# Freeing the buffers of split weights by half tiles, in a four-layer trunk on one core

## The chip, the cores and the metric

The kernel runs on one core of a Trainium2 chip. The metric is the device time of one launch in microseconds (us); the median of several runs is compared.

## The reference, cut to what matters

Four layers on a residual stream of 256 tokens by 1024 channels, float32. Each layer has a token mixer and then a conv-gated MLP:

```
for i in range(4):
    h = rms_norm(x, norm_mix[i])
    y = [dsa_mixer, rwkv7_mixer, s5_mixer][i % 3](h, ...)   # layers 0 and 3: dsa
    x = x + y
    h = rms_norm(x, norm_ffn[i])
    u = conv3(h @ w_up) + conv_b            # w_up: 1024 x 5632, causal depthwise, width 3
    gate, val = split(u); x = x + (silu(gate) * val) @ w_down   # w_down: 2816 x 1024
```

The DSA mixer projects queries, keys, values and an indexer (`dsa_w_in`), takes for each query the top 64 keys by indexer score, does attention over them with normed queries and keys, and projects with `dsa_w_out`.

## The kernel before

The residual is kept transposed, `xT`: 128 channels per block on partitions, 8 blocks, 256 tokens. Every weight matrix is walked in tiles of 1024 rows by 256 columns (`TILE`), that is two blocks (b = 0, 1) of 128 output channels and 8 chunks of the inner dimension. A tile fills one psum bank, block 0 the first half of it and block 1 the second. SyncE loads the tiles into a ring of three slots (`ring`, `send`, `wait_slot`).

Most weights are split in two fp32r parts, high and low, and a product is three matmuls (`product`, L386 to L390: high by high, high by low, low by high). The split is made on the chip, block by block:

- ScalarE copies the raw block to `w_high` (`round_weights`, L363), both blocks one after the other;
- VectorE subtracts for block 0 and GpSimd for block 1 into `w_low` (`rest_of_weights`, L371), each when `w_rounded` of the block says so;
- TensorE waits for `w_split` of the block (`split_weights`).

There are two buffers for split tiles (`NSPLIT` = 2). So tile n + 2 overwrites the parts of tile n, and ScalarE waits until tile n is wholly multiplied (`wait_used`, mostly the semaphore `bank_full` of its psum bank). `ahead(split, eng, key, ...)` issues the split of the tile two after `key`. Every engine works in its own program order, which is written out by hand:

- In `project` and `mlp_pe` TensorE does block 0's eight chunks and then block 1's, 24 matmuls each. Where the inputs come one by one (`ready`, the first tile of a stage, and the first and third tile of an MLP) the blocks alternate chunk by chunk.
- The MLP's up tiles come in pairs j (gate tile h = 0, value tile h = 1). For each, `mlp_act` waits for the tile, scales it by the newest tap (L769) and then rounds the weights ahead; `mlp_dve` adds the other taps (L846), does the low part ahead of block 0, and after both tiles multiplies gate and value (L857). `mlp_pool` does block 1's low part and the low part of the inner activations (L798).
- The down stage has 4 column groups m with 3 row groups g each, 8, 8 and 6 chunks. In layer 1, VectorE computes tables for the next layer's S5 mixer between its low parts (`add_down`, `s5_tables`).
- In the DSA stage the tiles are i0, i1, an unsplit s, then k0 to k3, q0 to q3, v0 to v3, o0 to o3. ScalarE evicts each with a Square and a Copy behind the rounding (`evict_k`, `evict_q`, `evict_v`); TensorE needs the squares halfway through the next tile for the mean of each head (L954, L969). VectorE weighs the indexer's heads (L1238, L1240), finds the top keys (L1249, L1250, L1254), norms the keys (L1228, L1230), masks scores (L1265) and normalises (L1286), with the low parts at fixed places between. `project_tokens` does the value tiles with tokens as rows: both blocks of the weights are read by every product.
- `add_residual` adds an output tile to `xT` (L565), does a low part ahead, and prepares the input of the MLP (`split_early`, L429, `add_squares`, L440).
- At the start of a stage `norm_scale` (L483, L488) makes the normed input chunk by chunk, with ScalarE's `norm_round` (L503), and with a low part of weights after chunk 3.

Of the kernel before, what the change touches and what calls it, by code (L numbers as in the profile page):

```python
# [33 lines left out]
DC = D // P  # L34
# [76 lines left out]
class Plan:  # L111


    def __init__(self):
        self.tiles = []
        self.tile = {}
        self.used = {}
        self.split = {}
        self.split_tiles = []
        self.slot_dmas = [0] * NSLOT  # L120
        self.fills = [0] * NBANK
        self.bank = {}

    def weights(self, key, dmas=1, split=False):
        if split:
            self.split[key] = len(self.split_tiles)
            self.split_tiles.append(key)
        n = len(self.tiles)
        slot = n % NSLOT
        self.slot_dmas[slot] += 16 * dmas  # L130
        self.tiles.append(key)
        self.tile[key] = (n, slot, self.slot_dmas[slot])
# [51 lines left out]
def trunk(nc, A, out, layers=(0, 1, 2, 3)):  # L184
    plan = make_plan(layers)
    ctx = ExitStack()
    with ctx:
# [157 lines left out]

        def rows_of(key):
            return min(DC, FC - key[3] * DC) if key[1] == "down" else DC
# [7 lines left out]
        def round_weights(act, key, r=0):  # L355

            n = plan.split[key]
            w = landed(act, key, r)
            if n >= NSPLIT:
                wait_used(act, plan.split_tiles[n - NSPLIT], r)  # L360
            for b in range(2):
                raw, high, _ = split_part(key, b, w)
                act.activation(high, raw, ACT.Copy).then_inc(sem("w_rounded", b), 1)  # L363
# [152 lines left out]
        def project(pe, key, x, ready=None, halfway=None):  # L516
# [4 lines left out]
            for k, b in chunks_and_blocks(DC, ready):  # L521
# [7 lines left out]
                if key in plan.split:  # L529
                    mm = product(pe, out_, (parts[b][0][:, k, :], parts[b][1][:, k, :]), (x[0][:, k, :], x[1][:, k, :]),  # L530
                                 start, stop)
                else:
                    mm = pe.matmul(out_, parts[b][:, k, b * P:(b + 1) * P], x[:, k, :], start=start, stop=stop,  # L533
                                   skip_group_check=True)
# [25 lines left out]
        def add_residual(dve, L, s):  # L560

            for m in range(4):
                wait_full(dve, (L, s, m))
# [3 lines left out]
                if m < 3:  # L567
                    ahead(rest_of_weights, dve, (L, s, m), 0)
# [123 lines left out]
        def mlp_pe(pe, L):  # L692
# [3 lines left out]
            def pair(j, r):  # L696
                for h in range(2):
# [11 lines left out]
                    for c, b in chunks_and_blocks(DC, first):  # L709
                        if first and b == 0:  # L710
                            early_ready(pe, n, c) if j == 0 else wait_split_h(pe, n, c)
                        if b not in parts:
                            parts[b] = split_weights(pe, key, b, r)
                        mm = product(pe, banks[bank][:, b * T:(b + 1) * T], (parts[b][0][:, c, :], parts[b][1][:, c, :]),
                                     (high[:, c, :], low[:, c, :]), c == 0 and (b == 0 or not first), c == DC - 1)
                    mm.then_inc(sem("bank_full", bank), 1)
# [6 lines left out]
            for m in range(4):  # L723
                for g in range(3):
# [3 lines left out]
                    for b in range(2):  # L728
# [5 lines left out]
                        for k in range(kn):  # L734
# [8 lines left out]
                            else:  # L743
                                mm = product(pe, banks[bank][:, 0:T], (high[:, k, :], low[:, k, :]),
                                             (inner_high[:, c, :], inner_low[:, c, :]), first, last)
                        if g == 2:
                            mm.then_inc(sem("bank_full", bank), 1)
# [3 lines left out]
        def mlp_act(act, L):  # L751
# [5 lines left out]
            def pair(j, r):  # L757
# [3 lines left out]
                for h in range(2):  # L761
                    key = (L, "up", 2 * j + h)
                    if j:
                        wait_full(act, key, r)
                    else:
                        act.wait_ge(sem("scaled"), h + 1 + since("scaled", L))
# [5 lines left out]
                    if j:  # L772
                        ahead(round_weights, act, key, r=r)
# [48 lines left out]
        def mlp_dve(dve, L):  # L822
            def pair(j, r):
# [8 lines left out]
                for h in range(2):  # L832
                    bank = bank_of((L, "up", 2 * j + h))
# [16 lines left out]
                    if j:  # L850
                        ahead(rest_of_weights, dve, (L, "up", 2 * j + h), 0, r=r)
# [228 lines left out]
        def dsa_act(act, L):  # L1080
# [7 lines left out]
            def evict_k(i):  # L1088

                key = (L, "k", i)  # L1090
                wait_full(act, key)
                ahead(round_weights, act, key)
# [6 lines left out]
            def evict_q(g):  # L1099

                key = (L, "q", g)
                wait_full(act, key)
                ahead(round_weights, act, key)
# [14 lines left out]
            def evict_v(i):  # L1118

                key = (L, "v", i)  # L1120
                wait_full(act, key)
                ahead(round_weights, act, key)
# [1793 lines left out]
```

## Time and profile before

| | |
|---|---|
| runs | 1569.55, 1571.79, 1573.05 us; median 1571.79 |
| profiled execution | span 1570.8 us, first to last instruction; the profile gives no other time for it |
| TensorE busy | 1437.3 us, 92% |
| VectorE busy | 1073.6 us, 68% |
| ScalarE busy | 764.2 us, 49% |
| GpSimd busy | 643.2 us, 41% |
| DMA | 210.09 MB, mean 134 GB/s |
| mean granted TensorE clock | 0.966 |

PE is TensorE, DVE VectorE, ACT ScalarE, POOL GpSimd. The span of the profiled execution lies 1.0 us under the median of the runs. Matmuls are pipelined, so that TensorE's busy time counts more than the array's work, and a short wait between two of them doesn't show as idle time. A row of a timeline gives the start, the duration (of all that it merges, x2 for two), the engine, the line and the operation, and in brackets the idle time of the engine before it with what ended it.

### The profile page before, as it was taken

Reading aid. Unit: us, or ns where it says so; the run is one execution under the profiler, and the core shown is the slowest. Engines: PE = TensorE matmul, PEld = TensorE weight load, DVE = VectorE, ACT = ScalarE, POOL = GpSimd, SP = SyncE. Lnnn points to the kernel's source line nnn. Section 1 sums busy time; section 2 is a strip of 40 time slices with the busy share of each in tenths; the row PEclk is TensorE's granted clock in tenths of the full one; section 3 lists DMA queues with packets and bytes.
Section 4 is the critical chain, followed back from the end, with each engine's and each line's share of the span. In section 5 each row is a group of like instructions: output and inputs, shape, how many; then the busy total and the mean of one; then the engine's idle time right before and its main releaser. Section 6 shows DMA issues by size and latency. Waiting matters only on the chain.

```text
span 1570.8 us, 32850 instructions
## 1 busy us (share of the span) xinstructions
PE 1437.3 (92%) x13742; PEld 1344.1 (86%) x13742; DVE 1073.6 (68%) x1635; ACT 764.2 (49%) x1229; POOL 643.2 (41%) x319
## 2 busy tenths in 40 slices
PE   6989999999999888999997547999999898999998
PEld 5888999988787777999987547999989788999998
DVE  6496677743585556877798995687744598577652
ACT  4358565542251334655643103565655357565542
POOL 5232357752005203487640001457664232257753
PEclk8899999999999999999999768999999999999999
DMA  5443445553434002475551002545555343445553
GB/s 160 137 134 106 134 162 188 181 191 112 134 109 134 5 4 66 151 215 187 173 170 61 1 1 82 162 161 188 187 168 180 123 135 108 134 148 177 186 194 101
DMA packets 212053, 210.09 MB, mean 134 GB/s; under 512 B 12098, under 2 KB 211058, under 8 KB 211922
## 3 DMA queue, kind: packets, MB, share of 16 engines
q1 hardware_dynamic: 210784, 206.65, 40.9%
q0 software_dynamic: 800, 1.46, 0.5%
q8 instruction: 99, 1.62, 0.5%
q14 instruction: 32, 0.26, 0.1%
q10 hardware_dynamic: 338, 0.10, 0.0%
HBM read 207.15 MB, written 1.05 MB: 133 GB/s over the span
## 4 chain that ended last, share of the span: by engine, by line
PE 68%; DVE 23%; ACT 5%; issue 3%; POOL 1%; DMA 0%; ACTq 0%; DVEq 0%; SPq 0%; POOLq 0%
PE psum L388 14%; PE psum L390 13%; PE psum L389 13%; PE psum L739 7%; PE psum L533 5%; DVE work L2394 4%; DVE w_low L371 4%; PE psum L741 3%; ACT w_high L363 3%; DVE x_low L488 1%; DVE work L483 1%; DVE work L1228 1%; DVE work L846 1%; PE psum L1596 1%; PE psum L1610 1%
## 5 line engine op out<-in xcount | busy, mean ns | idle before, releaser
L371 POOL TENSOR_TENSOR w_low<-ring,w_high 128x1024 fp32r<-128x1024 f32 (+1 forms) x185 | 512.9, 2773 | 791.6 <-ACT w_high L363 746.9
L388 PE MATMUL psum<-x_high,w_high 128*128 128x256 f32 x1856 | 533.3, 287 | 14.6 <-DVE w_low L371 9.7
L389 PE MATMUL psum<-x_low,w_high 128*128 128x256 f32 x1856 | 527.9, 284 | 0.0
L390 PE MATMUL psum<-x_high,w_low 128*128 128x256 f32 x1856 | 527.9, 284 | 0.0
L363 ACT ACTIVATE w_high<-ring 128x1024 fp32r<-128x1024 f32 (+1 forms) x368 | 362.1, 1035 | 215.0 <-PE psum L390 125.3
L388 PEld LDWEIGHTS psum<-x_high,w_high 128*128 128x128 f32 x1856 | 359.0, 193 | 21.3 <-issue 14.4
L389 PEld LDWEIGHTS psum<-x_low,w_high 128*128 128x128 f32 x1856 | 359.0, 193 | 1.0 <-issue 1.0
L390 PEld LDWEIGHTS psum<-x_high,w_low 128*128 128x128 f32 x1856 | 359.0, 193 | 0.0
L371 DVE TENSOR_TENSOR w_low<-ring,w_high 128x1024 fp32r<-128x1024 f32 x183 | 249.1, 1362 | 130.3 <-ACT w_high L363 130.0
L846 DVE SCALAR_TENSOR_TENSOR work<-psum,par,work 128x255 f32<-128x255 f32 (+1 forms) x352 | 145.0, 476 | 119.7 <-ACT work L769 119.6
L739 PE MATMUL psum<-inner,w_high 128*128 128x512 f32 x528 | 186.4, 398 | 2.6 <-DVE w_low L371 2.6
L769 ACT ACTIVATE work<-psum,par 128x256 f32<-128x256 f32 x176 | 89.3, 561 | 174.0 <-PE psum L390 174.0
L741 PE MATMUL psum<-inner,w_low 128*128 128x256 f32 x528 | 148.1, 280 | 0.0
L739 PEld LDWEIGHTS psum<-inner,w_high 128*128 128x128 f32 x528 | 99.1, 188 | 27.2 <-DVE w_low L371 2.3
L857 DVE TENSOR_TENSOR work<-work 128x512 f32<-128x512 f32 x44 | 118.4, 2690 | 0.4
L741 PEld LDWEIGHTS psum<-inner,w_low 128*128 128x128 f32 x528 | 99.7, 189 | 0.0
L533 PE MATMUL psum<-work,ring 128*128 128x256 f32 x384 | 85.9, 381 | 2.1 <-DVE work L1918 1.1
L533 PEld LDWEIGHTS psum<-work,ring 128*128 128x128 f32 x384 | 72.2, 190 | 16.0 <-DVE work L1918 3.7
L798 POOL TENSOR_TENSOR inner<-work,inner 128x512 f32 (+1 forms) x44 | 75.0, 1709 | 0.0
L2394 DVE TENSOR_TENSOR work<-work 128x32 f32<-128x32 f32 (+5 forms) x108 | 67.9, 628 | 4.3 <-ACT work L2200 1.4
L388 PE MATMUL psum<-early_high,w_high 128*128 128x256 f32 x192 | 55.8, 291 | 3.7 <-DVE work L2600 1.9
L389 PE MATMUL psum<-early_low,w_high 128*128 128x256 f32 x192 | 54.3, 283 | 0.0
(322 smaller groups left out, 2126.7 us busy)
## 6 DMA issues: line engine op xcount, KB each, us to landing
ring<-in_ffn_w_up_dram SPq DMA_DIRECT2D x88, 1024.0 KB, 5.1
ring<-in_ffn_w_down_dram SPq DMA_DIRECT2D x32, 1024.0 KB, 5.0
ring<-in_dsa_w_in_dram SPq DMA_DIRECT2D x28, 1024.0 KB, 5.3
ring<-in_ffn_w_down_dram SPq DMA_DIRECT2D x16, 768.0 KB, 4.3
ring<-in_rwkv_w_rkv_dram SPq DMA_DIRECT2D x12, 1024.0 KB, 5.0
ring<-in_dsa_w_out_dram SPq DMA_DIRECT2D x8, 1024.0 KB, 5.0
ring<-in_s_w_glu_dram SPq DMA_DIRECT2D x8, 1024.0 KB, 5.3
ring<-in_rwkv_w_out_dram SPq DMA_DIRECT2D x4, 1024.0 KB, 5.0
```

Source lines behind the costliest of these rows:

```text
L363: act.activation(high, raw, ACT.Copy).then_inc(sem("w_rounded", b), 1)
L371: eng.tensor_tensor(low, raw, high.bitcast(F32), ALU.subtract).then_inc(sem("w_split", b), 1)
L388: pe.matmul(out_, lhs[0], rhs[0], start=start, stop=False, skip_group_check=True)
L389: pe.matmul(out_, lhs[0], rhs[1], start=False, stop=False, skip_group_check=True)
L390: return pe.matmul(out_, lhs[1], rhs[0], start=False, stop=stop, skip_group_check=True)
L533: mm = pe.matmul(out_, parts[b][:, k, b * P:(b + 1) * P], x[:, k, :], start=start, stop=stop, skip_group_check=True)
L739: pe.matmul(banks[bank][:, :], high[:, k, :], inner[:, :, c, :], start=first, stop=False, skip_group_check=True)
L741: mm = pe.matmul(banks[bank][:, 0:T], low[:, k, :], inner_high[:, c, :], start=False, stop=last, skip_group_check=True)
L769: act.activation(conv[:, j % 3, h, b, :], bank_of(key)[:, b * T:(b + 1) * T], ACT.Identity, bias=col("ffn_conv_b", c + L * 2 * FC, r), sca ...
L846: dve.scalar_tensor_tensor(out=row, in0=bank[:, b * T:(b + 1) * T - lag], scalar=col("ffn_conv_w", c + (L * 3 + tap) * 2 * FC, r), in1=row ...
L857: dve.tensor_tensor(gated[:, j % 3], conv[:, j % 3, 0], conv[:, j % 3, 1], ALU.mult).then_inc(sem("gated_done"), 1)
L2394: then(dve.tensor_tensor(out_, x, y, op))
```

## The change

Three things change. The plan gives each split tile a number in a new count, `half`, save value tiles and the third row group of the down stage, and TensorE increments `tile_half` with the last product that reads block 0. `round_weights` takes the blocks to do; for block 0 it waits for `tile_half` of the tile two before (for the third row group of the down stage: for the psum bank of its block 0; for value tiles: for the whole tile, as before), and for block 1 for the whole tile. And the order on two engines is changed: in the up loop and in `evict_k`, `evict_q` and `evict_v`, ScalarE rounds block 0 ahead of its wait for the tile and block 1 behind it (in the up loop behind the scaled tap as well); in the up loop and in `add_residual`, VectorE does its low part ahead of the taps or of the addition rather than behind them.

```diff
@@ Plan.weights
+            if key[1] != "v" and key[1:2] + key[3:] != ("down", 2):
+                self.half[key] = len(self.half) + 1
@@ new helpers
+        def wait_half(eng, key, r=0):
+            if key in plan.half:
+                eng.wait_ge(sem("tile_half"), r * ROUND + plan.half[key])
+            elif key[1] == "down":
+                wait_full(eng, (key[0], "down", key[2], 0))
+            else:
+                wait_used(eng, key, r)
+        def half_done(key, mm, last_of_first):
+            if last_of_first and key in plan.half:
+                mm.then_inc(sem("tile_half"), 1)
@@ round_weights
-        def round_weights(act, key, r=0):
+        def round_weights(act, key, *blocks, r=0):
             n = plan.split[key]
             w = landed(act, key, r)
-            if n >= NSPLIT:
-                wait_used(act, plan.split_tiles[n - NSPLIT], r)
-            for b in range(2):
+            for b in blocks or range(2):
+                if n >= NSPLIT:
+                    (wait_used if b else wait_half)(act, plan.split_tiles[n - NSPLIT], r)
                 raw, high, _ = split_part(key, b, w)
                 act.activation(high, raw, ACT.Copy).then_inc(sem("w_rounded", b), 1)
@@ project (mlp_pe alike, with c for k; in the down stage on b == 0)
+                    half_done(key, mm, b == 0 and k == DC - 1)
@@ add_residual
+                if m < 3:
+                    ahead(rest_of_weights, dve, (L, s, m), 0)
                 wait_full(dve, (L, s, m))
...
-                if m < 3:
-                    ahead(rest_of_weights, dve, (L, s, m), 0)
@@ mlp_act, for each tile of a pair
                     if j:
+                        ahead(round_weights, act, key, 0, r=r)
                         wait_full(act, key, r)
...
                     if j:
-                        ahead(round_weights, act, key, r=r)
+                        ahead(round_weights, act, key, 1, r=r)
@@ mlp_dve, for each tile of a pair
+                    if j:
+                        ahead(rest_of_weights, dve, (L, "up", 2 * j + h), 0, r=r)
                     bank = bank_of((L, "up", 2 * j + h))
...
-                    if j:
-                        ahead(rest_of_weights, dve, (L, "up", 2 * j + h), 0, r=r)
@@ evict_k (evict_q and evict_v alike)
+                ahead(round_weights, act, key, 0)
                 wait_full(act, key)
-                ahead(round_weights, act, key)
+                ahead(round_weights, act, key, 1)
```

## Rows read from the trace of the kernel before

**Rows 1.** The page's busy times: engine, busy us, share of the span, instructions.

```profile
PE 1437.3 (92%) x13742; PEld 1344.1 (86%) x13742; DVE 1073.6 (68%) x1635; ACT 764.2 (49%) x1229; POOL 643.2 (41%) x319
```

**Rows 2.** The chain that ended last, 88 to 125 us: start, us, what.

```profile
88.62 3.23 DVE w_low L371
...
112.79 3.33 DVE w_low L371
```

**Rows 3.** Timeline of the up loop: start us, us, engine, line, operation, idle before.

```profile
216.66 1.02 ACT L769 ACTIVATE work<-psum,par 128x256 f32<-128x256 f32 x2 [2.78 <-PE psum L390]
...
222.43 1.02 ACT L769 ACTIVATE work<-psum,par 128x256 f32<-128x256 f32 x2 [2.84 <-PE psum L390]
...
225.05 1.22 DVE L371 TENSOR_TENSOR w_low<-ring,w_high 128x1024 fp32r<-128x1024 f32 x1
...
225.42 3.11 POOL L371 TENSOR_TENSOR w_low<-ring,w_high 128x1024 fp32r<-128x1024 f32 x1 [2.66 <-ACT w_high L363]
```

**Rows 4.** Timeline of the start of the MLP of layer 0, by engine.

```profile
197.79 0.36 PE L388 MATMUL psum<-x_high,w_high 128*128 128x256 f32 x1 [1.52 <-DVE w_low L371]
...
210.62 0.38 PE L388 MATMUL psum<-x_high,w_high 128*128 128x256 f32 x1 [0.73 <-DVE w_low L371]
...
190.60 2.01 ACT L363 ACTIVATE w_high<-ring 128x1024 fp32r<-128x1024 f32 x2 [2.46 <-PE psum L390]
...
192.69 2.41 POOL L371 TENSOR_TENSOR w_low<-ring,w_high 128x1024 fp32r<-128x1024 f32 x1 [3.19 <-ACT w_high L363]
...
192.95 2.43 DVE L488 TENSOR_TENSOR x_low<-work,x_high 128x256 fp32r<-128x256 f32 x1 [2.10 <-ACT x_high L503]
...
207.48 2.00 ACT L363 ACTIVATE w_high<-ring 128x1024 fp32r<-128x1024 f32 x2
...
209.35 1.21 DVE L371 TENSOR_TENSOR w_low<-ring,w_high 128x1024 fp32r<-128x1024 f32 x1
...
209.56 6.62 POOL L371 TENSOR_TENSOR w_low<-ring,w_high 128x1024 fp32r<-128x1024 f32 x2 [3.49 <-ACT w_high L363]
```

**Rows 5.** Timeline of TensorE in the DSA stage of layer 0.

```profile
57.53 1.10 PE L954 MATMUL psum<-work,mean_head 128*128 128x512 f32 x2 [0.37 <-ACT work L1096]
...
75.05 1.13 PE L954 MATMUL psum<-work,mean_head 128*128 128x512 f32 x2 [0.27 <-ACT work L1096]
...
106.42 0.72 PE L985 MATMUL psum<-work 64*128 64x128 f32 x8 [1.37 <-DVE work L1265]
...
116.99 0.66 PE L996 MATMUL psum<-ident,work 128*128 128x128 f32 x4 [1.88 <-DVE work L1286]
```

**Rows 6.** Timeline of ScalarE, VectorE and GpSimd in the DSA stage of layer 0.

```profile
62.89 2.01 ACT L363 ACTIVATE w_high<-ring 128x1024 fp32r<-128x1024 f32 x2 [2.04 <-PE psum L390]
...
86.31 2.01 ACT L363 ACTIVATE w_high<-ring 128x1024 fp32r<-128x1024 f32 x2 [2.26 <-PE psum L390]
...
64.10 1.22 DVE L371 TENSOR_TENSOR w_low<-ring,w_high 128x1024 fp32r<-128x1024 f32 x1
...
64.98 2.59 POOL L371 TENSOR_TENSOR w_low<-ring,w_high 128x1024 fp32r<-128x1024 f32 x1 [6.04 <-ACT w_high L363]
...
81.25 2.43 POOL L371 TENSOR_TENSOR w_low<-ring,w_high 128x1024 fp32r<-128x1024 f32 x1 [4.61 <-ACT w_high L363]
...
81.67 3.10 DVE L371 TENSOR_TENSOR w_low<-ring,w_high 128x1024 fp32r<-128x1024 f32 x1
...
103.05 2.24 DVE L1254 TENSOR_SCALAR work<-work 128x256 f32<-128x256 f32 x1
```

**Rows 7.** Timeline of layer 1: its up loop and its down stage.

```profile
691.81 0.39 PE L388 MATMUL psum<-x_high,w_high 128*128 128x256 f32 x1 [0.24 <-POOL w_low L371]
...
789.21 1.23 DVE L371 TENSOR_TENSOR w_low<-ring,w_high 128x1024 fp32r<-128x1024 f32 x1 [1.41 <-ACT w_high L363]
...
817.31 1.23 DVE L371 TENSOR_TENSOR w_low<-ring,w_high 128x1024 fp32r<-128x1024 f32 x1 [0.79 <-ACT w_high L363]
...
845.63 0.69 DVE L589 TENSOR_TENSOR xT<-xT,psum 128x512 f32<-128x512 f32 x1
```

More of the change, by code:

```diff
@@ L119, in __init__ @@
         self.split_tiles = []
+        self.half = {}
         self.slot_dmas = [0] * NSLOT
@@ L715, in pair @@
                                      (high[:, c, :], low[:, c, :]), c == 0 and (b == 0 or not first), c == DC - 1)
+                        half_done(key, mm, b == 0 and c == DC - 1)
                     mm.then_inc(sem("bank_full", bank), 1)
@@ L745, in mlp_pe @@
                                              (inner_high[:, c, :], inner_low[:, c, :]), first, last)
+                        half_done((L, "down", m, g), mm, b == 0)
                         if g == 2:
@@ L1101, in evict_q @@
                 key = (L, "q", g)
+                ahead(round_weights, act, key, 0)
                 wait_full(act, key)
-                ahead(round_weights, act, key)
+                ahead(round_weights, act, key, 1)
                 if g < 2:
@@ L1120, in evict_v @@
                 key = (L, "v", i)
+                ahead(round_weights, act, key, 0)
                 wait_full(act, key)
-                ahead(round_weights, act, key)
+                ahead(round_weights, act, key, 1)
                 act.activation(v_tok[:, :, i * TILE:(i + 1) * TILE],
```

## The prediction

> **What bounds the kernel now.** I read the page first. TensorE is busy for 92% of the span [rows 1], so at most 133 us of idle time is there to win, and I looked for where it sits. Next the timeline of the up loop [rows 3]. ScalarE starts the scaled tap of one tile at 216.66 us and of the next at 222.43: a tile of 48 products takes 5.76 us, 0.12 us a product. VectorE finishes the low part of block 0 at 226.3 (225.05 + 1.22) and GpSimd that of block 1 at 228.5 (225.42 + 3.11). TensorE takes them up at about 228.2 and 231.1. Nothing waits: in this loop weights are ready 1.9 to 2.6 us early, and readying them sooner is worth nothing. The same view, for TensorE alone and over the whole span, gives the places where it does wait. A row's "idle" understates them: a product is drawn 0.28 us long but they follow each other at 0.12, so an idle of x costs x + 0.16. The places are: the first tiles of each of the four MLPs [rows 4], the DSA stage of layers 0 and 3 [rows 5], one tile of layer 1's up loop and its down stage [rows 7]. In the DSA stage the chain that ended last runs through VectorE from 88.6 to 125 us, and its low parts of weights are steps of it, 3.2 and 3.3 us each [rows 2]; the instruction alone takes 1.2 [rows 6]. The RWKV and S5 cores hold most of the other idle time and the change doesn't touch them.
>
> **How VectorE and GpSimd meet.** This decides the DSA stage. GpSimd's low part takes 2.4 us. Where VectorE's falls into it (81.67 in a GpSimd run from 81.25 to 83.68) it ends 1.08 us after GpSimd does [rows 6]: it waited, and then ran. So do its tensor_scalar at 103.05 (2.24 us) [rows 6] and its x_low at 192.95 (2.43 us, behind GpSimd's run from 192.69) [rows 4]. In the other direction GpSimd's 3.11 us at 225.42 holds the 0.75 us that VectorE still had to run [rows 3]. Each such meeting costs the later one up to 2.4 us. The Trainium skill (SBUF — State Buffer, "SBUF: two separate sides") says the two share a port pair as an exclusive lock, which goes for a whole instruction to whichever starts first. That speaks against counting the change as free, since it moves GpSimd's runs.
>
> **The change, part by part.** No instruction of work is added or removed; one semaphore increment rides on an existing product, and one wait takes the place of another.
>
> *ScalarE's block 0 leaves the end of a tile.* Its two copies took 2.00 us for both behind the tile's end. Block 0 now starts at half of the tile, 2.88 us earlier, when ScalarE is idle; block 1 starts 0.95 earlier than it did, and with it GpSimd. In the up loop and in the down stages of layers 0, 2 and 3 this adds slack where there was slack: 0 us. If that cover were gone (a low part over 2 us late) it would cost what is over; nothing in the rows comes near. SP frees a ring slot when both low parts are done, about 1 us sooner; loads are not waited for now, so 0.
>
> *Start of an MLP, third tile (197.79, idle 1.52).* Tile 0 interleaves its blocks, so block 0 ends only three products, 0.36 us, before the tile. ScalarE starts at 190.24 rather than 190.60, GpSimd at 192.33 rather than 192.69, VectorE's x_low waits for it as before, and all behind moves by 0.36. Bounds: 0 to 0.5. Four MLPs: 1.4; the first index tiles of the two DSA layers have the same form: 0.7. Sum 2.1 us.
>
> *Start of an MLP, fifth tile (210.62, idle 0.73, so 0.9 lost).* VectorE's low part stands behind the four taps of the third tile and runs from 209.35. Now ScalarE rounds block 0 before the two instructions of its tap (0.9 to 1.0 us, as in [rows 3], just ahead of its 207.48), so from 206.58 to 207.6, and VectorE's part ends at 208.9; TensorE comes at 209.6 and doesn't wait. Block 1 is what is late next: ScalarE has it at 209.5 as before, GpSimd runs 209.6 to 212.0 (its run was longer because VectorE's low part held it), and TensorE wants it at 212.4. It holds by 0.4. The taps start some 1.3 us later; their readers aren't near. Gain 0.9 × 4 = 3.6, bounds 0.5 × 4 and 0.9 × 4 [rows 4].
>
> *Layer 1, 691.81 (idle 0.24).* GpSimd was late with block 1, after its own DMA issues; it starts its chain 1 us earlier: 0.4 [rows 7].
>
> *Layer 1's down stage.* VectorE computes S5 tables between the low parts and ends the stage (addition at 845.63). It waited for ScalarE's rounding 1.41 us at 789.21 and 0.79 at 817.31 [rows 7]. ScalarE's block 0 is 1 us earlier at the first and far earlier at the second: 1.0 + 0.8, and one meeting with GpSimd gets 0.2 shorter: 2.0. Bounds: 0.5 (one whole meeting more on this chain would take 2.4 of it, less what it moves) to 3.
>
> *DSA, key and query tiles.* The head means wait for ScalarE's copies behind the rounding: idle 0.37 once and 0.27 four times [rows 5]. One copy of 1 us leaves that queue, against 0.43 to 0.53 lost, so all five close: 0.53 + 4 × 0.43 = 2.25 us a layer, if nothing else fills them. Something does. VectorE is the slower engine here, so I follow its order. Logits come 0.53 earlier, and it is ready for the low part of k1's successor at 63.57 (64.10 before). GpSimd, at 64.98 before, moves by 0.53 and by the 0.95 of the one copy, to 63.49 [rows 6]. It takes the port 0.08 us ahead and VectorE is done at 67.0, 1.7 later than now. The next low part meets GpSimd's 72.6 to 75.0 and ends at 76.1. Weighing then starts at 79.2, just as GpSimd's run for q1 does (79.3), and its products wait for 81.95; it ends at 85.75, and q1's low part at 86.9. TensorE wants q1 at 84.8 (q0 ends just before ScalarE's 86.31 now, and 0.53 and two times 0.43 are won by then): a stall of 2.2 us that wasn't there. From here TensorE is 0.85 later than before. But the meetings that VectorE had at 88.62, 7.3 later and at 103.05 change: the first is gone (90.85 to 92.0), the second ends at 99.2 as before, the third at 104.4 rather than 105.3. The wait for the mask at 106.42 (1.37) shrinks and TensorE is 0.9 earlier; a shorter meeting before the wait at 116.99 brings 0.4 more. So 1.3 a layer, 2.6 for both. Value tiles keep their wait for the whole tile, and the output tiles run without idle time: 0. Bounds: −2.4 a layer (one more meeting on the chain than counted, with the 1.3 lost half) and +4.5.
>
> The Trainium skill's rule would give the same here, to whoever is first: by it the two are 0.08 us apart, and no row decides between them with more than that. If it went the other way the sum would be the case B below.
>
> **The sum.** 2.1 + 3.6 + 0.4 + 2.0 + 2.6 = 10.7 us off the profiled span of 1570.8: 1560.1. The median of the runs, 1571.8, stands 1.0 above that span, so 1561.1; I give 1561.0.
>
> **Rivals.**
> A, the above: 1561.0.
> B, *VectorE gets in first at 63.5.* Then its low part ends at 64.7 and it is 2.3 ahead; weighing is cut by one run of GpSimd, q1's low part ends at 83.5 (wanted at 84.8, no stall), two later meetings remain, and the mask is ready at 103.35 rather than 106.4. The five gaps and most of the wait at 106.42 are kept: 3.4 a layer. 8.1 + 6.9 = 15: 1556.8; if the later waits for masks close too, a further 1 a layer, 1554.8. For it: only 0.08 us stands against it, less than ScalarE's or TensorE's hand-over times vary between rows. Against it: both layers have the same spacing, so it has to tip twice.
> C, *the late part becomes another.* At the fifth tile GpSimd's block 1 has 0.4 us to spare; if VectorE's next low part holds it, the 0.9 is lost again (−3.6). The S5 tables meet one more run of GpSimd (−2.0), and the DSA chain gives back its 2.6. What is left is 2.5: 1569.3, no measurable change. In favour: six meetings are near at hand in rows 4 and 6. Against: three independent places must fail.
> D, *slower.* One mechanism: in the DSA stage GpSimd's run, now 1 us after the tile's end rather than 2, falls on VectorE's weighing of the second query half, on the low part before it and on that behind it, in each round. A lost port is 2.4 us, and VectorE sets this stage. To cancel 10.7 and cost 3 more, each layer must lose about 7 us, three meetings more than in A. Time then 1575. For it: the sequence has a dozen such instructions and I count margins of 0.1 us. Against: a VectorE that is late passes into stretches where GpSimd is idle for 4.6 us and more, which limits how many it can lose.
> E, *the change doesn't act*, because block 0 is still rounded behind the tile: excluded for single-block order, and true for the interleaved tiles, where I count only 0.36.
>
> **How the numbers follow.** A 0.47, B 0.31, C 0.13, D 0.09. What a measurement of this kernel can tell from no change is 0.2%, 3.1 us, so 1568.6 is the border: faster holds A, B and a part of C's spread, 0.82; same 0.11; slower 0.07. The range goes from B's lower end with a little beyond (1554) to C's edge (1568.5); below it lies some of B, above it C and D, together under 2 in 10. A's own range is 1558 to 1565.
>
> **What the profile after would show.** Right: TensorE's idle before the fifth tile of each MLP gone, the third tile's down to 1.16; ScalarE's L363 as single instructions, one at half of a tile and one at its end; the gaps before the head means gone; in layer 1's down stage VectorE without a wait for L363 at 817 and its last addition about 2 us earlier against the stage's start. For A: TensorE waits about 2.2 us for q1's low part. For B: it doesn't, and the wait at 106.42 is 0.6. Wrong would be: new waits of TensorE on GpSimd's low part at an MLP's fifth tile, or low parts of VectorE over 3 us at more places in the DSA stage than the five of now.

## The result

The changed kernel takes 1559.68 us (median of 4 runs, 1558.62 to 1562.13) against 1571.0 before. The ratio is 0.992, with a 95% interval of 0.9903 to 0.9936: 0.8% faster. The prediction said 1561.0. The profiled execution took 1560.63 us with a span of 1558.9, 11.9 less than before, with a mean granted clock of 0.963.

Line numbers move: `round_weights` is L380, `rest_of_weights` L388, `product` L405 to L407, the scaled tap L790, the other taps L869; the kernels of the experiments have numbers a few lines off these. First the page's busy times, to be read against [rows 1], and two of its groups (busy us, mean ns of one, then idle time before and its releaser), with the same two groups of the kernel before at the end:

```profile
PE 1436.8 (92%) x13742; PEld 1346.4 (86%) x13742; DVE 1099.2 (71%) x1635; ACT 772.5 (50%) x1229; POOL 585.2 (38%) x319
...
L388 POOL TENSOR_TENSOR w_low<-ring,w_high 128x1024 fp32r<-128x1024 f32 (+1 forms) x185 | 454.3, 2456 | 836.0 <-ACT w_high L380 791.4
...
L388 DVE TENSOR_TENSOR w_low<-ring,w_high 128x1024 fp32r<-128x1024 f32 x183 | 302.3, 1652 | 154.3 <-ACT w_high L380 153.2
```

```profile
L371 POOL TENSOR_TENSOR w_low<-ring,w_high 128x1024 fp32r<-128x1024 f32 (+1 forms) x185 | 512.9, 2773 | 791.6 <-ACT w_high L363 746.9
...
L371 DVE TENSOR_TENSOR w_low<-ring,w_high 128x1024 fp32r<-128x1024 f32 x183 | 249.1, 1362 | 130.3 <-ACT w_high L363 130.0
```

GpSimd is 58 us less busy and VectorE 26 us more. No work moved between them; the time in which one holds the other is drawn as busy time of the one that is held. More often now it is VectorE: its low parts grew by 53 us and GpSimd's shrank by 59, while VectorE's products of gate and value, less held than before, went from 118.4 to 80.6 us. At most places nothing is late for it.

The start of layer 0's MLP, TensorE, ScalarE, VectorE and GpSimd in turn, to be read against [rows 4]:

```profile
191.41 0.36 PE L405 MATMUL psum<-x_high,w_high 128*128 128x256 f32 x1 [1.17 <-DVE w_low L388]
...
200.21 1.04 ACT L380 ACTIVATE w_high<-ring 128x1024 fp32r<-128x1024 f32 x1
...
202.06 2.00 ACT L380 ACTIVATE w_high<-ring 128x1024 fp32r<-128x1024 f32 x2
...
201.41 1.22 DVE L388 TENSOR_TENSOR w_low<-ring,w_high 128x1024 fp32r<-128x1024 f32 x1
...
204.11 2.58 DVE L388 TENSOR_TENSOR w_low<-ring,w_high 128x1024 fp32r<-128x1024 f32 x1
...
203.19 2.42 POOL L388 TENSOR_TENSOR w_low<-ring,w_high 128x1024 fp32r<-128x1024 f32 x1 [3.49 <-ACT w_high L380]
```

The third tile waits 1.17 us instead of 1.52, and the fifth no longer waits: its low part of block 0 is done at 202.6, ahead of the taps. The next one, at 204.11, starts inside GpSimd's run and takes 2.58, and nothing is late for it.

Further into the up loop, VectorE and GpSimd, to be read against [rows 3]:

```profile
243.18 2.31 DVE L388 TENSOR_TENSOR w_low<-ring,w_high 128x1024 fp32r<-128x1024 f32 x1
...
247.83 1.71 DVE L388 TENSOR_TENSOR w_low<-ring,w_high 128x1024 fp32r<-128x1024 f32 x1 [0.78 <-ACT w_high L380]
...
246.05 2.41 POOL L388 TENSOR_TENSOR w_low<-ring,w_high 128x1024 fp32r<-128x1024 f32 x1 [1.65 <-ACT w_high L380]
```

Here GpSimd holds VectorE's low part in every tile: it takes 2.31 and 1.71 us in turn, where it took 1.22 before. It stands ahead of the taps now, and ends 4.1 and 5.9 us before TensorE takes up its tile (245.49 for about 249.6, 249.54 for about 255.4), where it was 1.9 us before. So these meetings cost nothing.

The DSA stage of layer 0, TensorE, VectorE and GpSimd, to be read against [rows 5] and [rows 6]:

```profile
53.29 1.02 PE L975 MATMUL psum<-work,mean_head 128*128 128x512 f32 x2
...
82.96 0.36 PE L405 MATMUL psum<-x_high,w_high 128*128 128x256 f32 x1 [2.15 <-DVE w_low L388]
101.41 0.72 PE L1006 MATMUL psum<-work 64*128 64x128 f32 x8 [0.43 <-DVE work L1289]
111.39 0.66 PE L1017 MATMUL psum<-ident,work 128*128 128x128 f32 x4 [1.27 <-DVE work L1310]
...
59.79 3.41 DVE L388 TENSOR_TENSOR w_low<-ring,w_high 128x1024 fp32r<-128x1024 f32 x1
...
75.75 5.61 DVE L1264 SCALAR_TENSOR_TENSOR work<-work 128x256 f32<-128x256 f32 x7
...
81.59 1.22 DVE L388 TENSOR_TENSOR w_low<-ring,w_high 128x1024 fp32r<-128x1024 f32 x1
...
59.72 2.41 POOL L388 TENSOR_TENSOR w_low<-ring,w_high 128x1024 fp32r<-128x1024 f32 x1 [5.50 <-ACT w_high L380]
...
75.46 2.50 POOL L388 TENSOR_TENSOR w_low<-ring,w_high 128x1024 fp32r<-128x1024 f32 x1 [4.22 <-ACT w_high L380]
```

This is case A. The head means don't wait (no bracket at 53.29). GpSimd starts 0.07 us ahead of VectorE at 59.7, and VectorE's low part ends 1.07 us after GpSimd's. That puts the weighing (75.75) behind GpSimd's next run, q1's low part ends at 82.8, and TensorE waits 2.15 us for it. Layer 3 has the same row at 1264.49, also 2.15.

Layer 1's down stage, TensorE and then VectorE, against [rows 7]:

```profile
789.58 0.50 PE L758 MATMUL psum<-inner,w_high 128*128 128x512 f32 x1 [0.83 <-DVE w_low L388]
...
823.21 0.39 PE L405 MATMUL psum<-inner,w_high 128*128 128x256 f32 x1 [0.94 <-DVE w_low L388]
...
762.62 1.65 DVE L869 SCALAR_TENSOR_TENSOR work<-psum,par,work 128x255 f32<-128x255 f32 x4 [1.29 <-ACT work L790]
...
811.10 1.23 DVE L388 TENSOR_TENSOR w_low<-ring,w_high 128x1024 fp32r<-128x1024 f32 x1
...
833.95 0.69 DVE L607 TENSOR_TENSOR xT<-xT,psum 128x512 f32<-128x512 f32 x1
```

Where the 11.9 us came from, with each boundary the start of a row in both traces (the first row of the s tile, the first head mean, the first product of each MLP and of layer 1's mixer, the first taps of the last up tile, the last addition):

| stretch | before | after | difference |
|---|---|---|---|
| start to layer 0's s tile | 34.75 | 34.09 | −0.66 |
| to its first head mean | 22.78 | 19.20 | −3.58 |
| rest of its DSA mixer | 126.09 | 124.32 | −1.77 |
| MLP of layer 0 | 203.57 | 202.22 | −1.35 |
| layer 1's mixer and up loop | 384.16 | 382.79 | −1.37 |
| layer 1's down stage | 74.28 | 71.33 | −2.95 |
| layer 2's mixer | 168.53 | 167.99 | −0.54 |
| layer 2's MLP, to layer 3's s tile | 211.48 | 211.16 | −0.32 |
| to its first head mean | 19.69 | 21.73 | +2.04 |
| rest of its DSA mixer | 126.07 | 125.98 | −0.09 |
| MLP of layer 3, to the end | 199.4 | 198.09 | −1.31 |

Two of these are not the change's work but the clock's. The windows of the two stretches from s tile to head mean, before and then after (the last three columns are the granted clock as a share of 2.4 GHz, the DMA share and GB/s):

```profile
34.75:57.53 22.78, 22.41 (x123) 20.84 (x123) 4.72 (x5) 4.28 (x9) 6.75 (x4) 0.72 0.44 140
1225.64:1245.33 19.69, 19.33 (x122) 18.21 (x123) 5.88 (x8) 6.39 (x11) 3.54 (x2) 0.84 0.52 161
```

```profile
34.09:53.29 19.20, 19.20 (x122) 18.27 (x123) 4.66 (x5) 4.31 (x9) 7.82 (x7) 0.83 0.52 164
1213.10:1234.83 21.73, 21.73 (x123) 20.56 (x123) 5.79 (x8) 6.39 (x11) 3.97 (x2) 0.73 0.47 146
1004.00:1006.00 2.00, 2.00 (x11) 2.00 (x11) 1.75 (x3) 1.97 (x3) 0.00 (x0) 0.50 0.00 0
1266.00:1268.00 2.00, 2.00 (x12) 2.00 (x11) 1.86 (x7) 0.00 (x0) 0.59 (x1) 0.50 1.01 350
```

In both layers TensorE waits 4.2 to 5.0 us ahead of the s tile, in both kernels, and then runs a part of the stretch at 1.2 GHz (in the kernel before, the granted clock is 0.50 from 34 to 40 and from 46 to 50). A stretch of t us at a granted clock c lacks t(1 − c) us of full clock: layer 0's 6.4 before and 3.3 after, layer 3's 3.2 and 5.9. That is −3.1 and +2.7 of the table's −3.58 and +2.04; what is left is −0.5 and −0.7, the head mean's wait of 0.53 that is gone. The same stretch with the same work differs by 3 us between two layers of one execution, so this is not to be credited to the change, and over both layers it nearly cancels.

### The profile page after: what moved, and what is told of

Same layout as the page of the kernel before. It is cut to its first block, busy times and chain, and to the rows that moved or that the text cites. A ratio compares the mean times of both kernels' runs of the same rounds, so it can differ in the third digit from the quotient of the medians.

```text
span 1558.9 us, 32946 instructions
## 1 busy us (share of the span) xinstructions
PE 1436.8 (92%) x13742; PEld 1346.4 (86%) x13742; DVE 1099.2 (71%) x1635; ACT 772.5 (50%) x1229; POOL 585.2 (38%) x319
## 4 chain that ended last, share of the span: by engine, by line
PE 73%; DVE 22%; ACT 3%; issue 2%; DMA 0%; ACTq 0%; DVEq 0%; SPq 0%
PE psum L405 16%; PE psum L407 15%; PE psum L406 15%; PE psum L758 6%; PE psum L551 5%; DVE work L2418 4%; PE psum L760 3%; DVE w_low L388 3%; DVE x_low L505 2%; DVE work L500 1%; DVE work L1252 1%; ACT w_high L380 1%; DVE work L1264 1%; PE psum L1620 1%; PE psum L1634 1%
## 5 line engine op out<-in xcount | busy, mean ns | idle before, releaser
L388 POOL TENSOR_TENSOR w_low<-ring,w_high 128x1024 fp32r<-128x1024 f32 (+1 forms) x185 | 454.3, 2456 | 836.0 <-ACT w_high L380 791.4
L405 PE MATMUL psum<-x_high,w_high 128*128 128x256 f32 x1856 | 532.9, 287 | 12.9 <-DVE w_low L388 9.5
L407 PE MATMUL psum<-x_high,w_low 128*128 128x256 f32 x1856 | 527.8, 284 | 0.0
L380 ACT ACTIVATE w_high<-ring 128x1024 fp32r<-128x1024 f32 (+1 forms) x368 | 376.8, 1037 | 224.1 <-PE psum L407 132.6
L388 DVE TENSOR_TENSOR w_low<-ring,w_high 128x1024 fp32r<-128x1024 f32 x183 | 302.3, 1652 | 154.3 <-ACT w_high L380 153.2
L405 PEld LDWEIGHTS psum<-x_high,w_high 128*128 128x128 f32 x1856 | 358.8, 193 | 18.6 <-issue 13.9
L407 PEld LDWEIGHTS psum<-x_high,w_low 128*128 128x128 f32 x1856 | 358.8, 193 | 0.0
L869 DVE SCALAR_TENSOR_TENSOR work<-psum,par,work 128x255 f32<-128x255 f32 (+1 forms) x352 | 144.6, 472 | 46.7 <-ACT work L790 46.5
L790 ACT ACTIVATE work<-psum,par 128x256 f32<-128x256 f32 x176 | 89.3, 561 | 131.7 <-PE psum L407 131.7
L878 DVE TENSOR_TENSOR work<-work 128x512 f32<-128x512 f32 x44 | 80.6, 1831 | 6.9 <-DVE work L869 5.1
L405 PE MATMUL psum<-early_high,w_high 128*128 128x256 f32 x192 | 56.4, 294 | 3.5 <-DVE work L2624 1.9
L407 PE MATMUL psum<-early_high,w_low 128*128 128x256 f32 x192 | 55.0, 287 | 0.0
```

Source lines behind the costliest of these rows:

```text
L388: eng.tensor_tensor(low, raw, high.bitcast(F32), ALU.subtract).then_inc(sem("w_split", b), 1)
L405: pe.matmul(out_, lhs[0], rhs[0], start=start, stop=False, skip_group_check=True)
L407: return pe.matmul(out_, lhs[1], rhs[0], start=False, stop=stop, skip_group_check=True)
L790: act.activation(conv[:, j % 3, h, b, :], bank_of(key)[:, b * T:(b + 1) * T], ACT.Identity, bias=col("ffn_conv_b", c + L * 2 * FC, r), sca ...
L869: dve.scalar_tensor_tensor(out=row, in0=bank[:, b * T:(b + 1) * T - lag], scalar=col("ffn_conv_w", c + (L * 3 + tap) * 2 * FC, r), in1=row ...
L878: dve.tensor_tensor(gated[:, j % 3], conv[:, j % 3, 0], conv[:, j % 3, 1], ALU.mult).then_inc(sem("gated_done"), 1)
```

## The experiments

Eight kernels in two groups, each timed in five rounds beside the kernel before: its median was 1571.95 in the first group (1 to 4), 1570.62 in the second (5 to 8).

### 1. ScalarE's half alone

The changed kernel with VectorE's order of before.

```diff
@@ add_residual and mlp_dve
-                    if j:
-                        ahead(rest_of_weights, dve, (L, "up", 2 * j + h), 0, r=r)
                     bank = bank_of((L, "up", 2 * j + h))
                     ...
+                    if j:
+                        ahead(rest_of_weights, dve, (L, "up", 2 * j + h), 0, r=r)
```

> The changed kernel with VectorE's order of before: low parts behind taps and additions, ScalarE as changed. My theory: VectorE's order matters only at the fifth tile of each MLP (0.9 us each), so this is 3.6 us slower than the changed kernel, about 1563.3, with the idle of 0.7 before the fifth tile back. Rival, that order is worth nothing (block 0 rounded earlier by ScalarE is enough): 1559.7.

Measured: 1585.51 us (1582.36 to 1591.07), ratio 1.0093 (1.0076 to 1.0111). This was missed by 22 us and on the wrong side: half of a change that wins 0.8% loses 0.9%. Its timeline, TensorE at the fifth tile, then ScalarE, VectorE and GpSimd in the up loop:

```profile
208.73 0.38 PE L405 MATMUL psum<-x_high,w_high 128*128 128x256 f32 x1 [3.18 <-DVE w_low L388]
...
216.28 1.02 ACT L790 ACTIVATE work<-psum,par 128x256 f32<-128x256 f32 x2 [1.88 <-PE psum L407]
...
228.06 1.02 ACT L790 ACTIVATE work<-psum,par 128x256 f32<-128x256 f32 x2 [1.97 <-PE psum L407]
...
224.66 2.92 DVE L388 TENSOR_TENSOR w_low<-ring,w_high 128x1024 fp32r<-128x1024 f32 x1
...
224.08 2.42 POOL L388 TENSOR_TENSOR w_low<-ring,w_high 128x1024 fp32r<-128x1024 f32 x1 [3.35 <-ACT w_high L380]
```

ScalarE now has block 1 a microsecond sooner, so GpSimd starts at 224.08 while VectorE is at its taps, and VectorE's low part at 224.66 takes 2.92 us and not 1.22. In [rows 3] it was VectorE that started first, by 0.37 us. Without VectorE's new order, the 1.9 us by which TensorE had its weights early are used up: a pair of tiles takes 11.78 us (228.06 − 216.28) instead of 11.52 (two of 5.76), and the fifth tile waits 3.18, in the other layers 3.20, 3.20 and 3.21. Ten pairs of 0.26 and one wait of 3.2 + 0.16 are 6.0 us an MLP, 24 for four, where the two profiled spans differ by 24.6 (1583.5 and 1558.9).

### 2. VectorE's half alone

The kernel before, with VectorE's low parts ahead of taps and additions as in the change, nothing else.

```diff
@@ add_residual and mlp_dve, on the kernel before
+                    if j:
+                        ahead(rest_of_weights, dve, (L, "up", 2 * j + h), 0, r=r)
                     bank = bank_of((L, "up", 2 * j + h))
                     ...
-                    if j:
-                        ahead(rest_of_weights, dve, (L, "up", 2 * j + h), 0, r=r)
```

> The kernel before with VectorE's new order alone: low part ahead of taps and additions, ScalarE still rounds both blocks behind the tile and its tap. The low part then waits for the rounding with the taps behind it. Theory: the fifth tile comes about 0.7 us sooner in each MLP, nothing else moves: 1571.0 - 2.8 = 1568.2. Rival: the taps, held by the wait, are the next thing late and it is slower than before, above 1572.

Measured: 1567.74 us (1565.94 to 1569.72), ratio 0.9977 (0.9968 to 0.9986), as expected. The fifth tile's wait is gone in all four MLPs, the third tile's stays at 1.52, and the waits in layer 0's DSA stage and in layer 1's down stage are within 0.25 us of those before. So the fifth tile's term of the sum belongs to VectorE's order alone.

### 3. The DSA mixer's rounding as before

The changed kernel, with both blocks rounded behind the wait for the tile in the three evictions.

```diff
@@ evict_k, evict_q, evict_v
-                ahead(round_weights, act, key, 0)
                 wait_full(act, key)
-                ahead(round_weights, act, key, 1)
+                ahead(round_weights, act, key)
```

> The changed kernel, but in the DSA stage ScalarE rounds both blocks behind the whole tile as before; MLPs and their down stages as changed. Theory: the DSA stages' net gain is lost, 2.6 us by the prediction (3.4 between the two profiles), so 1562.3 to 1563.1, without the 2.2 us stall of TensorE at q1. Rival, the DSA stages gained nothing net but a chance difference in TensorE's clock: 1559.7 or below.

Measured: 1562.03 us (1558.12 to 1566.39), ratio 0.9933 (0.992 to 0.9946). q1's stall is gone, the head means wait again (0.28, then 0.19 four times) and the mask too:

```profile
73.79 1.13 PE L975 MATMUL psum<-work,mean_head 128*128 128x512 f32 x2 [0.19 <-ACT work L1117]
...
104.82 0.71 PE L1006 MATMUL psum<-work 64*128 64x128 f32 x8 [1.28 <-DVE work L1286]
```

The medians put the DSA part of the change at 2.4 us for two layers, where the prediction had 2.6. The interval is wider than the effect (about 2 us to either side), so the time doesn't show it. The rows show which waits come back and that the stall goes, but not the net in us.

### 4. GpSimd second in the DSA stage

The changed kernel, ScalarE rounding block 1 behind its Square and Copy. It tests whether 0.07 us at 59.7 decides between cases A and B.

```diff
@@ evict_k and evict_q
                 ahead(round_weights, act, key, 0)
                 wait_full(act, key)
-                ahead(round_weights, act, key, 1)
                 ...
                                ACT.Copy).then_inc(sem("k_raw"), 1)
+                ahead(round_weights, act, key, 1)
```

> The changed kernel, but for key and query tiles ScalarE rounds block 1 behind its Square and Copy, so that GpSimd's run starts 1.0 us later and the head's mean 1.0 us sooner. Theory (GpSimd took the port 0.07 us ahead of VectorE at the low part behind the first weighing): now VectorE goes first, the stall of 2.15 us at q1 is gone, each DSA stage is about 2 us shorter: 1555.5. Rival: the meetings only move to other instructions and q1 is still late: 1559.7 within 1.

Measured: 1556.68 us (1556.46 to 1557.59), ratio 0.9909 (0.9897 to 0.9922); case B had been given 1556.8. VectorE and then GpSimd:

```profile
59.52 1.23 DVE L388 TENSOR_TENSOR w_low<-ring,w_high 128x1024 fp32r<-128x1024 f32 x1
```

```profile
60.34 2.66 POOL L388 TENSOR_TENSOR w_low<-ring,w_high 128x1024 fp32r<-128x1024 f32 x1 [5.53 <-ACT w_high L380]
```

VectorE starts first and is done in 1.23 us, GpSimd has to wait for it and takes 2.66, and q1's stall doesn't occur in either layer. But four later low parts of VectorE meet GpSimd (2.77 to 3.45 us each) and the masks are late again: TensorE waits 1.30, 1.87, 0.72, 0.37 and 1.10 us for them, nearly as in the kernel before. So this is case B's time, but not its path, in which most of the first of these waits had closed.

### 5. ScalarE's half alone, with GpSimd made the second

Kernel 1, where GpSimd waits in the up loop for VectorE's low part of the same tile. If the meeting is what costs kernel 1 these 24 us, they come back.

```diff
@@ mlp_pool, on kernel 1
+        def after_vector(pool, key, r=0):
+            pool.wait_ge(sem("w_split", 0), r * ROUND + plan.split[key] + 1)
...
                 for h in range(2):
+                    if j:
+                        ahead(after_vector, pool, (L, "up", 2 * j + h), r=r)
                     ahead(rest_of_weights, pool, (L, "up", 2 * j + h), 1, r=r)
```

> As e1 (VectorE's order of before, ScalarE as changed, 1585.5), but in the up loop from the second pair on GpSimd waits for VectorE's low part of the same tile before it does its own. Theory: e1 was slow because ScalarE's block 1, 1 us earlier, lets GpSimd start 0.6 us before VectorE comes from the taps, so that VectorE's low part takes 2.9 rather than 1.2 us and ends too late for TensorE, at the fifth tile and a little in every pair. With VectorE first it takes 1.2 again: the idle of 3.2 before the fifth tile falls to about 0.7 and the pairs to 11.52, so 1563 to 1566. Rival, the early half copies themselves (more waits on ScalarE) cost the time: stays near 1585.

Measured: 1564.53 us (1561.57 to 1570.15), ratio 0.9957 (0.9938 to 0.9975). TensorE at the fifth tile, VectorE and GpSimd in the loop:

```profile
207.68 0.38 PE L409 MATMUL psum<-x_high,w_high 128*128 128x256 f32 x1 [1.52 <-DVE w_low L388]
...
222.12 1.22 DVE L388 TENSOR_TENSOR w_low<-ring,w_high 128x1024 fp32r<-128x1024 f32 x1
...
223.41 2.78 POOL L388 TENSOR_TENSOR w_low<-ring,w_high 128x1024 fp32r<-128x1024 f32 x1 [3.36 <-DVE w_low L388]
```

21 us come back between the medians. VectorE's low part takes 1.22 again, GpSimd's starts only behind it, and the pace of the loop is restored (11.5 us a pair). The fifth tile waits 1.52 to 1.56 us in the four MLPs, where 0.7 was expected: ScalarE's copy of block 0 now stands ahead of the scaled tap, so VectorE's taps, and its low part behind them, come later: the low part starts 12.34 us after the third tile, where it was 11.56 in the kernel before. What is left to the changed kernel is the fifth tile: 1.52 + 0.16 us in each of four MLPs, 6.7 together; the medians stand 4.9 apart, and by the ratios it is 5.8.

### 6. The down stage's block 0 as before

The changed kernel; in the down stage ScalarE's block 0 waits for the whole tile two before.

```diff
@@ wait_half
-            if key in plan.half:
+            if key in plan.half and key[1] != "down":
                 eng.wait_ge(sem("tile_half"), r * ROUND + plan.half[key])
-            elif key[1] == "down":
-                wait_full(eng, (key[0], "down", key[2], 0))
             else:
                 wait_used(eng, key, r)
```

> The changed kernel, but in the down stages ScalarE's block 0 waits for the whole tile again. Theory: only layer 1's down stage, where VectorE waits for the rounding between the S5 tables, loses by it: the 2.0 of the prediction to the 2.9 between the two profiles, so 1561.7 to 1562.6. Rival: the stage got shorter by what VectorE and GpSimd no longer meet, not by the half tiles: 1559.7.

Measured: 1565.05 us (1562.27 to 1566.0), ratio 0.995 (0.9932 to 0.9967), 5.4 over the changed kernel and more than expected. VectorE and TensorE in layer 1:

```profile
768.75 1.65 DVE L867 SCALAR_TENSOR_TENSOR work<-psum,par,work 128x255 f32<-128x255 f32 x4 [1.29 <-ACT work L788]
...
819.88 3.38 DVE L386 TENSOR_TENSOR w_low<-ring,w_high 128x1024 fp32r<-128x1024 f32 x1
...
843.03 0.69 DVE L605 TENSOR_TENSOR xT<-xT,psum 128x512 f32<-128x512 f32 x1
...
832.29 0.39 PE L403 MATMUL psum<-inner,w_high 128*128 128x256 f32 x1 [2.96 <-DVE w_low L386]
```

From the taps of the last up tile to the last addition it takes 74.28 us, to the hundredth what the kernel before takes; the changed kernel takes 71.33. So the term is 2.95 us. Layer 0's MLP takes the same as in the changed kernel (189.67 and 189.68 us from the third tile to layer 1's mixer): a down stage without tables has slack for the whole tile. The rest of the 5.4 isn't this term: stretches that the edit doesn't touch differ by more than that, both ways. Layer 1's mixer is 4.7 us longer here: from its first products to the third tile of the MLP 268.83 us against 264.17, with a granted clock of 0.93 against 0.97 between its 120th and 220th us. Layer 3's is 3.7 shorter (143.99 against 147.71 us from the s tile to the MLP, with a clock of 0.96 against 0.94). Why a kernel draws a lower clock in one stretch stays open; kernels 5, 7 and 8 show 266.2, 268.3 and 267.6 us for the stretch in layer 1.

### 7 and 8. A VectorE order that leaves the meetings out

Kernel 4 and the changed kernel, both with VectorE's DSA program reordered: q1's low part (`split("k", 3)`, the tile two after k3) stands behind three of the four search rounds that follow the second weighing rather than ahead of them, so that GpSimd's run falls on search steps, which it doesn't hold, and the norm of k2 comes ahead of the first mask.

```diff
@@ dsa_dve
             weigh(1)
+            take(1, 3)
             split("k", 3)
-            take(1, 4)
+            take(1, 1)
             split("q", 0)
...
             scale_q(0)
+            k_norm(2)
             mask(0)
             split("q", 2)
             mask(1)
-            k_norm(2)
```

Kernel 7, on kernel 4:

> e4 (1556.7) and another order on VectorE in the DSA stage: the low part for q1 goes behind three of the four rounds of the top-k search that follow the second weighing, so that GpSimd's run lies under instructions that don't need the port, and the third norming of keys goes ahead of the first mask. Theory: three of the meetings of 2 us go, the first mask is ready before TensorE asks for it, and the waits for the masks (1.3 + 1.9 + 0.7 + 0.4 + 1.1 a stage) close for the most part: 4 us a stage, 1548.5. Rival: the normings moved ahead push the low parts for the value tiles late and TensorE waits for those: 1556 or above.

Kernel 8, on the changed kernel:

> The changed kernel with the order of e7 on VectorE, but ScalarE's block 1 ahead of the Square and Copy as in the changed kernel. Theory: GpSimd still goes first at the low part behind the first weighing (1.7 us late), and again in the second weighing, which ends at about 81.5; q1's low part now stands behind three more rounds of the search, so TensorE waits 5 us for q1. What follows gains as in e7. Together within 2 us of the changed kernel: 1560. Rival: the order alone carries all of e7's gain: 1549.

Measured: kernel 7 takes 1546.98 us (1544.08 to 1548.13), ratio 0.9832 (0.9813 to 0.9852), faster than both kernels. Kernel 8 takes 1559.82 (1559.08 to 1561.56), ratio 0.9921, which is the changed kernel's time. Kernel 7, VectorE, GpSimd and TensorE:

```profile
61.78 3.35 DVE L1252 RECIPROCAL work<-work 128x512 f32<-128x512 f32 x1
...
71.27 0.30 DVE L1273 MAX8 work<-work 128x8 f32<-128x128 f32 x1
...
73.48 3.61 DVE L1264 SCALAR_TENSOR_TENSOR work<-work 128x256 f32<-128x256 f32 x7
...
80.26 1.23 DVE L388 TENSOR_TENSOR w_low<-ring,w_high 128x1024 fp32r<-128x1024 f32 x1
```

```profile
61.46 2.66 POOL L388 TENSOR_TENSOR w_low<-ring,w_high 128x1024 fp32r<-128x1024 f32 x1 [5.53 <-ACT w_high L380]
70.59 2.38 POOL L388 TENSOR_TENSOR w_low<-ring,w_high 128x1024 fp32r<-128x1024 f32 x1 [6.47 <-ACT w_high L380]
77.20 2.38 POOL L388 TENSOR_TENSOR w_low<-ring,w_high 128x1024 fp32r<-128x1024 f32 x1 [4.22 <-ACT w_high L380]
```

```profile
114.34 0.71 PE L1006 MATMUL psum<-work 64*128 64x128 f32 x8 [0.98 <-DVE work L1289]
```

The reciprocal runs across GpSimd's 61.46 and MAX8 across its 70.59 at their usual lengths. GpSimd's run at 77.20 lies under the search rounds, and q1's low part behind it, at 80.26, takes 1.23 (3.34 in kernel 4). The seven weighing products take 3.61 us as in kernel 4, instead of the changed kernel's 5.61. All of VectorE's low parts in this stage take 1.2, and of the waits for masks one is left, 0.98. In kernel 8 GpSimd is first at 60.71 against VectorE's 60.79, so the whole order runs 2.3 us late and q1's stall grows:

```profile
86.90 0.55 PE L405 MATMUL psum<-x_high,w_high 128*128 128x256 f32 x1 [5.10 <-DVE w_low L388]
```

With kernel 4's later GpSimd the order is worth 9.7 us between the medians (12 by the ratios, 0.9909 and 0.9832); without it, nothing. The reordering makes two moves, of q1's low part and of a norm, and no kernel has one of them alone.

## Why the prediction was right, point by point

- **Third tile, 0.36 for each MLP:** 1.52 became 1.17. **Index tiles, 0.35 a layer:** TensorE's wait ahead of the s tile went from 5.04 to 4.69 in layer 3, and the stretch ahead of it in layer 0 is 0.66 shorter.
- **Fifth tile, 0.9 for each:** the wait is gone, and block 1 was not late (the margin of 0.4 held). MLPs of layers 0 and 3: −1.35 and −1.31, where 0.36 + 0.9 = 1.26 was predicted. Layer 2's came to −0.32 where 1.61 (with 0.35 of the index tile) was due: after the wait at its start the clock is at half from 1004 to 1006 and partly around it, some 1.7 us that the kernel before doesn't lose there.
- **Layer 1's 691.81, 0.4:** the wait is gone, but the stretch won 1.37, 0.3 less than the 1.66 due.
- **Layer 1's down stage, 2.0:** 2.95, shown by kernel 6. This term was mis-sized. The first part (1.0) is right: 1.86 of idle became 0.83. The second was given 0.8 and 0.2 for a shorter meeting, and was 2.0 (2.96 became 0.94): the meeting at 822.50 didn't get shorter but went away. Before, GpSimd started 0.10 us ahead of VectorE there (822.40 and 822.50); now VectorE starts 0.83 ahead (811.10 and 811.93).
- **DSA, 1.3 a layer:** the path of case A came true step by step as far as the wait at 111.39, with the stall at 2.15 for 2.2. That the size came out is in part luck. TensorE's idle time past the first head mean fell by 2.8 us in layer 0 and 1.3 in layer 3 (each wait with its 0.16), 3.4 and 1.8 with the first head mean's. In layer 0 two later waits for masks that the prediction left standing, 0.44 and 1.08 us (at 124.91 and 130.65 before), are gone; ahead of the second, GpSimd had started 0.09 us before VectorE's low part (126.23 and 126.32), which took 3.43 us, and now starts 1.0 behind it (121.98 and 120.98), and it takes 1.23. Against this, in each layer about 1.7 us more than before ran below full clock: at 112 to 120 in layer 0, in layer 3 at 1266 to 1270, right behind the new stall. With the first head mean's 0.53 that makes 1.6 and 0.2; by the table it is 2.3 and 0.6. The prediction's 1.3 lies between, and these 0.4 to 0.7 us are not accounted for. The other traces don't fix the size either. The stretch from the s tile to the MLP, both layers added, takes 294.6, 290.4 and 296.2 us with the DSA rounding of before (the kernel before, kernels 2 and 3) and 291.2, 287.9, 288.6 and 288.2 with the changed one (the changed kernel, 1, 5 and 6). That is 4.7 less on average, where 2.6 was predicted, but kernels with the same rounding lie up to 5.8 apart.
- **The up loop, 0 us and "nothing comes near":** the number held, but the reason left out a meeting. With block 1 a microsecond sooner, GpSimd holds VectorE's low part in every tile. Kernel 1 shows what that costs with VectorE's old order: its up loops take 24 us more than the changed kernel's, and all but some 7 of that come back in kernel 5, where the meeting is taken out. In the changed kernel the meetings are still there (2.31 and 1.71 us); what covers them is that VectorE's low part, ahead of the taps, has 4.1 or 5.9 us to spare. The prediction costed the two halves one by one and added them up; by themselves they are +14.6 (1.0093) and −3.6 us (0.9977), together −12.6 (0.992).
- **Rivals:** B's time is what kernel 4 gives, within 0.1 us, though by another path: VectorE goes first and q1 isn't late, but the waits for the masks stay. C and D needed meetings at places where none came.
- **The sum:** 11.9 us off the span for 10.7. By rows of the table the gain stands up to 3.1 us above and 2.6 below what was predicted for the row, mostly by the clock, and layer 2's mixer gave 0.54 that nothing predicts. These differences cancel for the most part, so the small error of the total is better than the terms were.

The lock of the Trainium skill (SBUF — State Buffer, "SBUF: two separate sides") agrees with every meeting shown here, down to a start 0.07 us ahead (59.72 and 59.79) and 0.08 (60.71 and 60.79). By the same section a VectorE instruction takes part with two inputs from SBUF or in a 2-port mode; a reciprocal and a MAX8, with one input, kept their 3.35 and 0.30 us beside GpSimd. One input alone is no safe sign: the tensor_scalar at 103.05 in [rows 6], with one, took 2.24 us inside GpSimd's run, where in layer 3 of the changed kernel, outside of one, it takes 0.29.

## What to carry to other kernels

When an edit makes one engine's instruction start earlier, list who shares a port with the engine that it feeds, and compare starts: who comes first decides who pays, and 0.1 us can decide over 2 us. Then ask whether the one that is held has time to spare: in the changed kernel's up loop it has, and the meeting is free; in kernel 1 it has not. Two halves of a change that act on both sides of such a pair are costed together, not added. And where one engine has instructions that the lock doesn't hold, put these where the other engine's long ones fall; here an order that does this, and moves one norm ahead of a mask, gained 9.7 us in kernel 7, nearly as much as the whole change.

## What the runs showed of the hardware

A VectorE low part that starts inside GpSimd's run ends 1.07 to 1.09 us after it, wherever in the run it started (59.79 and 204.11 here, as in [rows 6]); so it is in nearly all of some 400 such meetings in the ten traces. GpSimd, held by VectorE, pays no more than what VectorE had left (at 60.34 in kernel 4, 2.66 instead of 2.4 us, with 0.41 left), so here it was cheaper to let VectorE go first.

A wait of TensorE of 1 to 2 us is sometimes followed by a stretch at half clock, and sometimes not: behind the stall at 1264.49 the granted clock is 0.50 for two microseconds, about 1.7 us in all from 1266 to 1270, while the same stall at 82.96 in layer 0 was followed by full clock. Layer 2's MLP starts behind a wait of 1.91 us in both kernels, at full clock before and at half clock after. What decides it no run here shows. Stretches of identical work differ by 3 us between layers of one execution, with the lower granted clock in the longer one, so differences of this size have to be read in windows, with the clock beside them.
